# Residual stream kept with features on the partitions, root mean square factors applied when a product leaves PSUM, output projections giving features by tokens

## What is computed

```
h = rms_norm(x, g_mix_pre);  u = h @ w_in          # aq ak av cu rq rk rv rg
mix = concat[chunk_attention(aq, ak, av), conv_module(cu), retention(rq, rk, rv, rg)] @ w_out
x = x + rms_norm(mix, g_mix_post)
h = rms_norm(x, g_mlp_pre)
f = square(relu(h @ w_up)) @ w_down                # 4096 wide
x = x + rms_norm(f, g_mlp_post)
```

```
q, k, v, u, gates = split(rmsnorm(h, norm1_gain) @ w_in)
o = diff_attention(rope(rmsnorm(q)), rope(rmsnorm(k)), v, lam);  attn = rmsnorm(o) @ w_attn_proj
s = s5_layer(u, ...) @ w_ssm_proj                  # state space layer with 32 groups of 64 states
h = h + (sigmoid(g_attn) * attn + sigmoid(g_ssm) * s) @ w_out
up = causal_dwconv(rmsnorm(h, norm2_gain) @ w_up)  # 2 * 2816 wide, three taps
h = h + (silu(gate) * val) @ w_down
```

## Time and profile before

| | |
|---|---|
| median of 3 runs | 2409.61 us (2408.82 to 2410.8) |
| profiled execution | 2411.09 us, span 2409.3 us |
| mean granted TensorE clock | 0.965 of full |
| PE busy | 2242.4 us, 93% |
| PE weight load | 1734.9 us, 72% |
| DVE busy | 1090.2 us, 45% |
| ACT busy | 885.3 us, 37% |
| POOL busy | 816.8 us, 34%, 211 instructions |
| DMA | 197.14 MB, 24.6% of 16 engines' time |

### The profile page before, as it was taken

The page is one execution under the profiler, slowest core; times in us unless marked ns, Lnnn a source line. Parts: engine busy times, 40 slices in busy tenths (PEclk is TensorE's granted clock), DMA queues, the critical chain, the costliest instruction groups (busy, mean ns, idle before and its releaser), DMA issues.

```text
span 2409.3 us, 28514 instructions
## 1 busy us (share of the span) xinstructions
PE 2242.4 (93%) x10184; PEld 1734.9 (72%) x10184; DVE 1090.2 (45%) x1840; ACT 885.3 (37%) x1367; POOL 816.8 (34%) x211
## 2 busy tenths in 40 slices
PE   7999989999979998899999988876999799999999
PEld 6865578888868773778888776654766577877887
DVE  3643352323347344332332488784155642344434
ACT  4333453223242334532322342343255634333322
POOL 2422134444433320334444452421322133433343
PEclk9999989999989999999999988988999999999999
DMA  5412022232224211122322241111211122222231
GB/s 191 139 44 70 18 70 88 93 99 93 99 86 156 78 49 36 53 83 92 99 92 92 83 142 53 36 71 41 86 53 53 36 75 83 88 93 90 96 103 71
DMA packets 109724, 197.14 MB, mean 82 GB/s; under 512 B 4656, under 2 KB 41776, under 8 KB 109104
## 3 DMA queue, kind: packets, MB, share of 16 engines
q1 hardware_dynamic: 109616, 195.73, 24.6%
HBM read 191.52 MB, written 8.12 MB: 83 GB/s over the span
## 4 chain that ended last, share of the span: by engine, by line
issue 65%; POOL 16%; PE 15%; DVE 2%; ACT 1%; POOLq 0%; DVEq 0%; ACTq 0%
POOL w_lo L501 15%; PE bank L610 13%; PE bank L857 1%; POOL x L512 1%; PE bank L677 0%; DVE hid L2063 0%; ACT hid L1488 0%; DVE hid L2057 0%; DVE x L2039 0%; ACT h_hi L1154 0%; POOLq L162 0%; ACT act_hi L1137 0%; DVE b_pow L1849 0%; DVE b_pow L1846 0%; POOL cos_n L553 0%
## 5 line engine op out<-in xcount | busy, mean ns | idle before, releaser
L501 POOL TENSOR_TENSOR w_lo<-raw,w_hi 128x2048 fp32r<-128x2048 f32 (+1 forms) x170 | 756.3, 4449 | 1514.8 <-ACT w_hi L1104 1514.3
L610 PE MATMUL bank<-act_hi,w_hi 128*128 128x512 f32 x1520 | 625.0, 411 | 36.9 <-DVE act_lo L1554 25.5
L610 PE MATMUL bank<-act_lo,w_hi 128*128 128x512 f32 x1520 | 603.5, 397 | 0.0
L610 PE MATMUL bank<-act_hi,w_lo 128*128 128x512 f32 x1520 | 602.6, 396 | 0.0
L1104 ACT ACTIVATE w_hi<-raw 128x2048 fp32r<-128x2048 f32 (+1 forms) x170 | 314.1, 1847 | 760.5 <-PE bank L610 746.0
L610 PEld LDWEIGHTS bank<-act_hi,w_hi 128*128 128x128 f32 x1520 | 293.4, 193 | 113.7 <-issue 49.6
L610 PEld LDWEIGHTS bank<-act_lo,w_hi 128*128 128x128 f32 x1520 | 292.7, 193 | 67.7 <-issue 8.6
L610 PEld LDWEIGHTS bank<-act_hi,w_lo 128*128 128x128 f32 x1520 | 292.1, 192 | 63.4
L610 PE MATMUL bank<-w_hi,h_hi 128*128 128x512 f32 x688 | 273.1, 397 | 3.9 <-DVE x L2039 3.9
L610 PE MATMUL bank<-w_lo,h_hi 128*128 128x512 f32 x688 | 272.1, 396 | 0.0
L610 PE MATMUL bank<-w_hi,h_lo 128*128 128x512 f32 x688 | 272.0, 395 | 0.0
(11 more groups left out here) (295 smaller groups left out, 2477.6 us busy)
## 6 DMA issues: line engine op xcount, KB each, us to landing
raw<-in_w_up SPq DMA_DIRECT2D x32, 1024.0 KB, 5.2
raw<-in_w_down SPq DMA_DIRECT2D x32, 1024.0 KB, 5.0
raw<-in_w_in SPq DMA_DIRECT2D x26, 1024.0 KB, 5.1
raw<-in_w_up SPq DMA_DIRECT2D x44, 512.0 KB, 4.6
raw<-in_w_in SPq DMA_DIRECT2D x28, 768.0 KB, 4.5
raw<-in_w_out SPq DMA_DIRECT2D x12, 1024.0 KB, 5.0
raw<-in_w_down SPq DMA_DIRECT2D x22, 512.0 KB, 4.2
raw<-in_w_attn_proj SPq DMA_DIRECT2D x4, 1024.0 KB, 5.1
```

Source lines behind the costliest of these rows:

```text
L501: pool.tensor_tensor(m.w_lo[slot][:, 0:n], m.raw[slot][:, 0:n], m.w_hi[slot][:, 0:n].bitcast(F32), ALU.subtract).then_inc(s["split_ready"], 1)
L610: mm = pe.matmul(o, ll if i == 2 else lh, rl if i == 1 else rh, start=first and n == 0, stop=last and n == len(steps) - 1)
```

## The change

`x` is kept as `[P, KD, T]`, with features on the partitions (the host gives and takes it transposed). There are no diagonal matmuls. ACT and DVE split `x * gain` straight from SBUF, one block of 128 features at a time; the first group of products after a norm is made block by block into four banks (`first_group`), so that it can begin with the first block. ACT squares each block, POOL adds the squares up (six additions, `add_squares`), PE sums them over the partitions (`mean_columns`), ACT takes the root, DVE the reciprocal, PE spreads it over the partitions (`spread_rows`), and ACT keeps it as `rrow`. It is applied when products leave PSUM: by DVE (cu, up, the gates, u of the state space layer), by ACT as a scale (v), or later by POOL (`scale_rows`: q, k and the gate of the first block; `scale_group`: q and k of the second, 16 instructions). `w_out`, `w_down`, `w_out_2` and `w_down_2` are `feature_major`. The parameters of the state space layer are worked out at the start of the kernel. `lcol` is loaded behind the first column group's weights, once the arena is free.

```diff
-    def norm(base):
-        for t in range(NT):
-            pe.wait_ge(s["diag_ready"], c.up("diag_ready"))
...
-        emptied(*range(8))
+    def mean_columns(b):
+        fill(b)
+        pe.wait_ge(s["squares_added"], c.up("squares_added", KD - 2))
+        pe.wait_ge(s["squares_made"], c.up("squares_made", KD))
+        for t in range(NT):
+            for part, x in enumerate((m.sums, m.squares[(KD - 1) % 4])):
+                mm = pe.matmul(bank[b][:, t:t + 1], x[:, t * P:(t + 1) * P], m.per_d, start=(part == 0), stop=(part == 1))
+        mm.then_inc(s[f"full{b}"], 1)
...
+    def spread_rows(b, column):
+        fill(b)
+        pe.wait_ge(s["rstd"], c.up("rstd"))
...
+    def first_group():
...
+        for k in range(KD):
+            if k % KU == 0:
+                wh, wl = weights(next_unit(), KU, GROUP)
+            pe.wait_ge(s["act_lo"], c.up("act_lo"))
+            for b in range(4):
+                if k == KD - 1 and b == 0:
+                    mean_columns(MEAN_PRE)
+                if k == KD - 1 and b == 3:
+                    spread_rows(ROOT_PRE, m.rstd)
...
 # ACT
+    def pre_norm(gain, arrived=None, dmas=1, first=1, done=None):
+        for k in range(KD):
...
+            copy_hi(m.act_hi[:, k, :], m.x[:, k, :], scale=gain(k))
+            square(k, m.x[:, k, :])
+            if k == first:
+                hi(done, dmas=dmas)
+            if k == 5:
+                if arrived:
+                    parameters()
+                hi("half", dmas=dmas)
+        root(MEAN_PRE)
+        evac(ROOT_PRE, m.rrow[:])
...
 # DVE
+    def post_norm(post_gain, pre_gain, clear):
+        inverse(MEAN_POST, m.rstd_post)
+        full(ROOT_POST)
...
+        scale(0)
+        add(0)
+        for k in range(KD):
+            if k < KD - 1:
+                scale(k + 1)
+            split(k, pre_gain)
+            if k < KD - 1:
+                add(k + 1)
+        if clear:
+            link(dve.memset(m.f[:], 0.0))
+        root_row()
...
+    for k in range(KD):
+        if k == 6:
+            angles()
+        split(k, gain("g0", m.scol, SC))
+    powers()
+    root_row()
     dve.sem_inc(s["arena_free"], 1)
     layers(dve, c, layer)
...
 # POOL
+    def pre_norm():
+        add_squares(1, 2)
+        lo()
+        add_squares(3, 4, 5, 6)
+        lo()
...
+    def scale_group(x):
+        for b in range(4):
+            pool.wait_ge(s["in_ready"], c.up("in_ready"))
+            pool.tensor_tensor(x[:, b, :], x[:, b, :], m.rrow[:], ALU.mult).then_inc(s["in_scaled"], 1)
```

More of the change, by code:

```diff
@@ L308, in memory @@
     m.par = put("par", [P, N_PAR, NS])
-    m.prow = put("prow", [P, 2, D])
-    prow_at = top[0] - 8 * D
+    m.rrow = put("rrow", [P, T])
+    m.sin_t, m.cos_t = (put(f"turn_table{i}", [P, NS, TURN_A + TURN_B]) for i in range(2))
+    top[0] = (top[0] + 63) // 64 * 64
+    m.gate = put("gate", [P, 4, T])
+    late_at = top[0]
+    top[0] += 4 * 4 * T
     arena = (top[0] + 63) // 64 * 64
@@ L1281, in down @@
             use(4, 5, 6, 7)
+            if isinstance(g, int) and g == N_UP - 1:
+                for k in range(4):
+                    act.wait_ge(s["f_done"], c.up("f_done"))
+                    square(k, m.f[:, k, :])
             hi(7)
@@ L1470, in functions @@
         use(0, 1, 2, 3)
-    for t in range(NT):
-        freed(t)
-        root(m.x, t)
-    norm(4, gain("g2", m.scol, SC), *range(NT))
+    pre_norm(gain("g2", m.scol, SC), dmas=2, first=3, done=3)
     def column(g, b, tap):
@@ L1496, in up @@
         c.up("h_lo", 2)
-    last = N_UP2 - 1
     def down(g, i):
-        if not (isinstance(g, int) and g == last):
-            hi(dmas=2)
         use(4, 5, 6, 7)
@@ new lines, in arithmetic @@
+    dve.wait_ge(s["const_loaded"], 2 * 16)
+    dve.wait_ge(s["eps_loaded"], 16)
+    for k in range(KD):
+        if k == 6:
[3 more added lines that the diff above has]
+    root_row()
+    dve.sem_inc(s["arena_free"], 1)
+    layers(dve, c, layer)
+    par = m.par
+    for b in range(4):
+        full(b)
+        dve.tensor_tensor(m.uT[:, b, :].rearrange("p (j n) -> p j n", j=SUB), in_order(bank[b][:]), in_order(m.rrow[:]),
+                          ALU.mult).then_inc(s[f"free{b}"], 1)
+        freed(b)
+        dve.sem_inc(s["u_ready"], 1)
@@ L1993, in arithmetic @@
             for b in range(4):
-                use(b)
+                full(b)
+                gate = m.gates[:, 4 * g + b, :] if g < 2 else m.gate[:, b, :]
+                dve.tensor_tensor(gate, bank[b][:], m.rrow[:], ALU.mult).then_inc(s[f"free{b}"], 1)
+        if i >= 12 and i % 8 == 4:
+            g = i // 8 - 1
+            for b in range(4):
+                wait("gate_ready")
                 if g >= 2:
-                    wait("gate_ready")
                     branch = m.ssm[:, 4 * (g - 2) + b, :]
-                    dve.tensor_tensor(branch, branch, bank[b][:], ALU.mult).then_inc(s[f"free{b}"], 1)
+                    ins = dve.tensor_tensor(branch, branch, m.gate[:, b, :], ALU.mult)
+            if g >= 2:
+                link(ins)
         if 1 <= i <= n_steps:
@@ L2053, in up, with scale, taps @@
     def up(g, i):
-        for b in range(4):
-            use(b)
+        def scale(b):
+            full(b)
+            dve.tensor_tensor(bank[b][:], bank[b][:], m.rrow[:], ALU.mult).then_inc(s["up_scaled"], 1)
+        def taps(b):
             wait("tap0")
@@ L2059, in up @@
                                      ).then_inc(s[f"free{b}"], 1)
+        before = not isinstance(g, int) or g
+        scale(0)
+        for b in range(1, 4):
+            scale(b)
+            taps(b - 1)
+        if before:
+            add_to_x(4, 0)
+        taps(3)
+        if before:
+            add_to_x(5, 1)
         for b in range(2):
```

750 lines of the change are left out of this document (397 added, 353 removed).

## The result

The changed kernel takes 2447.69 us (median; 2446.46 to 2452.53), the one before in the same comparison 2409.22: a ratio of 1.0164, 95% interval 1.0146 to 1.0181. It is slower by 38 us, where 8 less were forecast, and beyond the slow rival's 2432. The profiled execution has a span of 2450.7 us against 2409.3; it is the longest of the changed kernel's four (2452.53, the others 2446.46 to 2448.56), so its stages add up to some 3 us more than the medians.

What follows compares the result with a forecast made beforehand. PE, busy 93% of the span, was taken to bound the kernel. Terms 8 + 8.5 − 17 − 0.5 + 8.4 + 3 − 2.5 = 7.9 us off 2409.6 gave 2401.7, likeliest 2401.5; whole range 2368 to 2430.

Steps and rivals of the forecast that it cites:

- slow rival: Rival: POOL blocks DVE on the critical path in norms and q/k scalings, nothing from swap or boundaries; 2432 us, chance 0.25.
- The four norms inside the layers: Layer norms: first product 11 us earlier, much given back in blocks; 2 us gained each, 8 in all.
- bad bound: Layer norms: second group 44.9 us after the last product if a w_lo stands just ahead of the last act_lo.
- The second block: Second block: parameter chain leaving gains 4.5, POOL's q and k scalings cost 5; −0.5 us together.
- The sign named for this: Second block: prediction is wrong if POOL's scalings put PE's gaps at q and k above today's.
- The gates pass over DVE: Under the rest: the gates' passing over DVE was put at −2 us.
- The swapped operands: down and half of w_out_2: streaming h or sum parts spaces products 0.2294 instead of 0.2333; 8.4 us gained.
- the sign that the prediction named: MLPs: down's spacing should be 0.229; the prediction is wrong if it keeps 0.233.
- The step's own doubt, the place of h: Swapped operands: h's place, not its role, may cost the spacing; range 0 to 14.3 us.
- The start: Kernel start: first product sooner, but parameter chain and late lcol delay the second group from 50.0 to 67; −17 us.
- The norm ahead of the second MLP: Before the second MLP: first product within 1 us of the last, clock kept; 8.5 us gained, bounds 5 and 11.
- Boundaries of the second MLP: Second MLP: idle and slow first products at ten group boundaries, 5.5 in all; +3 us, −3 to +5.5.

Runs made afterwards that it cites:

- e3: Changed kernel with POOL's additions of squares left out, the root taken over two of eight blocks; 2437.20 us, ratio 1.0112.
- e6: Changed kernel with the scaled block put in a PSUM bank, so the addition to x reads only one operand from SBUF; 2444.31 us, ratio 1.0118.
- e10: e6 with, around the four layer norms, the second unit's rounding ahead of the blocks and the next unit's w_lo behind the last act_lo; 2421.24 us, ratio 1.0034.
- e9: Changed kernel with POOL's 16 scalings of q and k in the second block left out; 2442.35 us, ratio 1.0124.
- e2: Changed kernel with the arena given free earlier, behind the last act_lo and ahead of the reciprocal; 2442.07 us, ratio 1.0130.
- e4: Changed kernel with the second block's gates leaving PSUM as before, without their row factor; 2442.07 us, ratio 1.0133.
- e13: Kernel before with only the operands of both MLPs' down products swapped; 2406.52 us, ratio 0.9982.
- e8: Changed kernel with only addresses changed, the arena with the MLP's h parts at the low end of SBUF; 2450.18 us, ratio 1.0124.
- e14: Kernel before with only addresses changed, the arena first; 2401.74 us, ratio 0.9961.
- e1: Changed kernel with the 35 steps of the powers moved from the start to the second block; 2445.94 us, ratio 1.0145.
- e15: e11 with the whole parameter chain back in the second block instead of the powers alone; 2416.07 us, ratio 1.0031.
- e11: e10 combined with e1 and e2: its norm order, powers in the second block, early arena signal; 2415.23 us, ratio 1.0017.
- e12: e11 with the arena at the low end of SBUF; 2402.91 us, ratio 0.9962 against the kernel before.
- e7: e2 with DVE's two layers one behind the other instead of in a hardware loop; 2458.82 us, ratio 1.0171.

## Why the prediction was wrong, by its own steps

- **"The four norms inside the layers (2 us each, 8 in all)."** This step failed. Its parts were right: first product at 8.0 (8.6), DVE's block 2.2 us when nothing holds it (2.1), the lock. Its bad bound, 44.9 us to the second group, was not bad enough: 47.7. Too small in the sum were the holds: the step names the six additions among the blocks, but its bounds reckon only with a `w_lo`, where each addition makes DVE's 2.2 us a block 1.1 longer. Missing was the price of a wait ahead of the last block, which is paid twice: 3.9 us, and then the lower clock for the mean's eight rows of matmuls and nine products. "It decides from the point where a POOL pass precedes a DVE pass that PE waits for in more than about one block in four": it was six blocks in eight of a middle norm, and two `w_lo` more. e3 and e6 show the hold, and e10 that its removal is worth 12 us a middle norm. The first end norm gave 1.7 us, near the forecast's 2, which is luck: it costs 5.9 in e9, where nothing in it was changed.
- **"The second block (−0.5 us)."** The largest miss: it cost some 16 by estimate (14.0, with an end norm in it, taken to give 1.7 as at the first layer's end). Two things stood in the sum and were sized wrongly. POOL's scalings cost 8 (e9), between the 5 taken and the 21 of the bound. The late table transfers cost 6.3 (e2) where the step gave the absent chain 4.5 of gain: taking the chain off DVE gains nothing when DVE then waits 10.26 us for a transfer. The sign named for this, longer gaps of PE at q, came (6.60 us against 2.21), but not by the scalings: the gap is the same without them.
- **"The gates pass over DVE (−2)."** 9.1 (e4), in an attention whose stretch costs 11.4. The step took the gates' 16 passes (0.69 us each, 11 in all) as lying beside other work, and they cost nearly their whole time. Whether as DVE's load or through the `w_lo` holds that they shift onto passes that PE waits for (L2130 in the rows above) is open. The remaining 2.3 us I did not pursue.
- **"The swapped operands (8.4 us)."** Zero in the changed kernel: h streamed still takes 0.233, the sign that the prediction named. The step took the spacing to go with h's role alone, and the change moves the arena, with h in it, as well. In the placement of before the role does pay, 0.229 streamed against 0.233 held (e13, 4.7 us); in the changed kernel's placement 0.233 is left with h streamed; with the arena first it is 0.227 in either role (e8, e14). The step's own doubt, the place of h, was thus half of the case. The Trainium skill (TensorE: Matmul & The Clock Gate, "NX overlap") gives 216 ns for 512 columns, as one figure. By it neither role nor place pays; the trace does not agree, with 227, 229 and 233 ns for one shape.
- **"The start (−17 us)."** Right in sign and size, and in most of the mechanism: 19.2, of which the powers 6.5 (e1), the angles 8.5 (e15 against e11) and the late `lcol` 2.3 (e2). But 7.3 go as well when POOL's additions do (e3), in part the same microseconds: the step has no hold of `act_lo` by the additions.
- **"The norm ahead of the second MLP (8.5 us)" and "Boundaries of the second MLP (+3 us)".** 5.7 and 5.0: right in kind, one low, one high. The group's boundary before (0.77 us from product to product and 0.33 to the next, 0.6 more than two usual ones, in each of eight groups of the stretch) is gone, 5 us in all.

The slow rival had the right mechanism, POOL's passes holding DVE's, and its 2432 is low in part by its own sum: it says that nothing comes from the swap or the boundaries, but leaves their 8.4 and 3 us in. Without them it is 7.9 − 14 − 16 − 11.4 = −33.5, so 2443, near the 2447.7 measured. That is still partly luck. It put 21 us on the scalings and the boundaries at nothing; the scalings cost 8 and the boundaries gave 5, while the attention cost 9.1 and the late transfers 6.3, of which it has nothing. The range of the whole forecast, to 2430, ended below this rival's own time. The Trainium skill (SBUF — State Buffer, "SBUF: two separate sides") says that only a DVE pass of two SBUF operands (or in a mode that uses both ports) is held by a GpSimd pass that reads SBUF, and then for its whole length. By that rule the trace agrees, and e6 shows its useful side: 1505 ns with both operands in SBUF, 680 with one of them in PSUM.

The change as made can be mended to within 0.2% of before (e11, ratio 1.0017), and with other addresses it is 0.4% faster than before (e12, 0.9962). But the kernel before gains as much from the addresses alone (e14, 0.9961). So nothing here shows that the new layout itself is worth time; its gains in the norms are used up by the start, the second block and the gates.

## What to carry to other kernels

When work moves to an engine with spare time, ask what else that engine holds while it works: 0.7 us passes became 1.8 and 4.1 us passes because POOL, idle two thirds of the time, had something to do at the wrong moment. Put a helper engine's long passes by an explicit wait behind the pass that must not be held, or let that pass read one operand from PSUM. And take the price of a pass from the stage in which it stands: DVE has 29 us more to do in the second MLP than before (138 against 109), and the stretch got 5 us shorter; in the attention 11 us more cost 9.

## What the runs showed of the hardware that was not expected

- A one-column float32 matmul (two records, the x2 of its row) costs PE as much as one of 512 columns in a rounded type: 0.22 us apart at the higher clock (366.40 to 366.62), 0.43 at the lower.
- The same 128x512 product comes 0.227, 0.229 or 0.233 us apart, depending on addresses in SBUF and on which operand streams. The addresses alone are worth 9.5 us (e14, 2064 products of h).
- After a loop's back edge DVE issued its first pass 8.6 us after its last, and 5.4 us after the last thing that it waits for was there (e2); without the loop on DVE it was 0.07 us (e7).
- With PE busy for 22.85 of 24 us, the granted clock stayed at its lower level (0.50) for all of them in e7; in e2 it was 0.86 over the same window. What makes the difference is not known.
- Two engines that start such passes 0.02 us apart settle which of them is held, and 7.6 us of the kernel with it.
